# ScalarE's tanh of the last merge tile, moved ahead of the next tile's first attention step

## The chip, the cores and the metric

One core of one Trainium2 chip runs the whole program. The metric is the device time of one execution in microseconds, from first to last instruction with what lies around it. The time before is the median of three runs.

## What is computed

Four transformer blocks run one after the other on one sequence of 512 tokens with 1024 features: two layers of a first kind, then two of a second kind. Only the mixer of the second kind matters here. Cut to that:

```python
def hybrid_mixer_2(h, ...):
    q_nsa, kv_nsa, g_nsa, qkv_sb, g_merge = split(h @ w_in)       # one wide input product
    o_nsa = nsa_attention(...)     # compressed blocks + selected blocks + window, softmax
    o_sb = stick_breaking_attention(...)
    g_a, g_b = split(sigmoid(g_merge), 2)
    y = g_a * (o_nsa @ w_proj_nsa) + g_b * (o_sb @ w_proj_sb)
    return y @ w_out

def stick_breaking_attention(q, k, v):       # for blocks of 128 queries
    z = q @ k.T * scale
    log_1m = where(strict, -softplus(z), 0)
    later = reversed_cumsum(log_1m) - log_1m
    w = where(strict, exp(log_sigmoid(z) + later), 0)
    out = w @ v
```

The kernel computes sigmoid(g) as half of 1 + tanh(g / 2): ScalarE stores the tanh in `gm`, the merge stage adds the 1 and the factor 0.5.

## The kernel before, in words

**Weights.** All weight matrices come as a stream of tiles of 128x1024. SP's queue loads a tile into a ring of four (`raw`). Products are done in three passes over pairs of rounded numbers: ScalarE copies half a tile into a rounded head `wh` (`head`, L171), GpSimd subtracts that from the raw weights for the residual `wl` (`rest`, L182), and TensorE does head x head, head x low, residual x head (L199 to L201). `wh` and `wl` hold two tiles, so the head of tile t+2 can be written, half by half, only when TensorE is done with that half of tile t (`slot_done`).

**The second mixer.** Its input product has 48 tiles (`for t in range(IN2)` in each engine's function). The last 16, t = 32 to 47, are the merge gates. Each fills a bank of 128x512 in PSUM, 4 or 5 by turns. When a merge tile t-1 is complete, VectorE multiplies its bank in place by the inverse norm (`weigh`, L2412), and ScalarE then takes the tanh into `gm` (`gate`, L2188), which frees the bank for tile t+1.

**Attention between the tiles.** Attention is cut into 52 steps: softmax attention, then four steps of the compressed blocks, then 16 stick-breaking steps. A tile has two slots, one behind its first and one behind its second half, and each slot does a part of several steps: TensorE computes the scores of step n (L2006), the transposes of the weights of step n-2 (L2027) and the values of step n-3 (L2060). In its slot n ScalarE copies the transposed weights of n-2 to SBUF (L2171), which frees banks 2 and 3, and computes two pairs of Sigmoids of the scores of n (L2149 and L2152), whose second of each pair frees score bank 0 or 1. GpSimd masks these (L1930), VectorE scans them (L2317) and multiplies (L2324). The stick-breaking steps lie in the slots of tiles 36 to 43; tile 44 has transposes, copies and values of the last two. A copy in a slot waits also for the values of n-3.

**What sets the order.** Each engine's order is written out in program order and each waits by semaphores. TensorE's iteration t is: claim the bank, first half, slot, second half, slot. VectorE's is: `weigh(t - 1)`, slot, slot, with splits of finished attention features inside the slots. ScalarE's iteration t is: first head of tile t+2, first slot, second head, tanh of merge tile t-1, second slot. The tanh waits for `inverted`, which `weigh` raises, and from the 14th merge tile on also for all stick-breaking products.

Of the kernel before, what the change touches and what calls it, by code (L numbers as in the profile page):

```python
# [203 lines left out]
def build(nc, a, out):  # L204
# [1612 lines left out]
    def second_mixer(sems, t0, joint):  # L1817
# [8 lines left out]
        kinds = MIX2_KINDS  # L1826
# [87 lines left out]
        def head_col(k, one):  # L1914
            _, tb, kind, p = steps[k]
            return 16 * tb + 8 * kind + soft_head(one, p)[2]
# [211 lines left out]
        def scalar(act):  # L2128
            def soften(k):
                kind, tb, one_, p = steps[k]  # L2130
                w_ = (tb + 1) * P
                if kind == "cmp":
                    act.wait_ge(cshift, tb + 1)
                    act.activation(csb[:, tb, :, 0:NCMP], csb[:, tb, :, 0:NCMP], ACT.Exp, scale=HD ** -0.5)\
                       .then_inc(cexp, 1)
                    return
                for one in range(2):
                    i = first_item[k] + one
                    if kind == "soft":
                        at = head_col(k, one)  # L2140
                        act.wait_ge(bank_free[one], score_use[k, one])
                        act.activation(prs[i % 6][:, 0:w_], prs[i % 6][:, 0:w_], ACT.Exp, bias=mins[:, at:at + 1],
                                       scale=-1.0, accum_out=den[:, at:at + 1]).then_inc(weights, 1)
                        continue
                    n = 2 * (k - CMP) + one
                    act.wait_ge(score, i + 1)
                    if n >= 3:
                        act.wait_ge(products, n - 2)
                    act.activation(lgs[n % 3][:, 0:w_], ps[one][:, 0:w_], ACT.Sigmoid, scale=-(HD ** -0.5))\  # L2149
                       .then_inc(keeps, 1)  # L2150
                    act.wait_ge(turned, i - 5)
                    act.activation(prs[i % 6][:, 0:w_], ps[one][:, 0:w_], ACT.Sigmoid, scale=HD ** -0.5)\  # L2152
                       .then_inc(bank_free[one], 1)

            def copies(k):
                kind, tb, _, p = steps[k]
                w_ = (tb + 1) * P
                if kind == "cmp":
                    act.wait_ge(turned, first_item[k] + 1)
                    if tb >= 2:  # L2160
                        act.wait_ge(pv, first_item[k] - 1)
                    act.activation(ptc[tb % 2][0:NCMP, 0, :], ps[2][0:NCMP, :], ACT.Copy).then_inc(bank_free[2], 1)
                    return
                for one in (range(2) if kind == "sb" else (1,)):
                    i = first_item[k] + one
                    act.wait_ge(turned, i + 1)
                    if k == CMP:
                        act.wait_ge(pv, SOFT_ITEMS)
                    elif k:
                        act.wait_ge(pv, first_item[k - 1] + 2)  # L2170
                    act.activation(m.tmp[:, one, 0:w_], ps[2 + one][:, 0:w_], ACT.Copy)\  # L2171
                       .then_inc(bank_free[2 + one], 1)

            def slot(n):
                if 0 <= n - TURN_LAG < len(steps):
                    copies(n - TURN_LAG)
                if n < len(steps):
                    soften(n)
                if n == GELU_TURN:
                    act.wait_ge(gelu_in, 1)  # L2180
                    act.activation(gt[:], gu_[:], ACT.Tanh).then_inc(gelu_out, 1)

            def gate(t):
                c = kinds[t][1]
                act.wait_ge(inverted, c + 1)
                if c >= 13:
                    act.wait_ge(products, 2 * 4 * NT)
                act.activation(gm[:, c, :], ps[bank_of[t]][:], ACT.Tanh, scale=0.5)\  # L2188
                   .then_inc(bank_free[bank_of[t]], 1)

            for t in range(IN2):
                kind, c = kinds[t]
                if t == 0:
                    joint.copy_inverse(act)
                else:
                    s.head(act, t0 + t + 2, 0)
                if (t, 0) in slots:
                    slot(slots[t, 0])
                s.head(act, t0 + t + 2, 1)
                if t and kinds[t - 1][0] == "merge":  # L2200
                    gate(t - 1)
                if kind == "svalue" and c == 3:
                    s.done(act, t0 + t)
                    for tb in range(2):
                        act.activation(sv2[:, tb, :], ps[tb][:], ACT.Identity, scale=xinv4[:, tb:tb + 1]).then_inc(bank_free[tb], 1)
                    act.wait_ge(bank_free[7], 1)
                    act.activation(gts_flat, vsw[:, :, 256:280], ACT.Tanh, scale=0.5).then_inc(gates, 1)
                if kind == "compress" and c % 4 == 3:
                    kv = c // 4
                    s.done(act, t0 + t)  # L2210
                    act.activation(raw_h[0:32, kv, :], ps[4 + kv][0:32, 0:P], ACT.Copy).then_inc(hidden_copied, 1)
                    act.wait_ge(hidden_copied, kv + 1)
                    act.sem_inc(bank_free[4 + kv], 1)
                if (t, 1) in slots:
                    slot(slots[t, 1])
            gate(IN2 - 1)

        def vector(dve):
# [198 lines left out]
            for t in range(IN2):  # L2417
# [26 lines left out]
                if (t, 1) in slots:  # L2444
                    slot(slots[t, 1])
            weigh(IN2 - 1)
        stage = Stage(sync, gpsimd, tensor, scalar, vector)
        stage.feat_ready = feat_ready
        return stage
# [449 lines left out]
```

## Time and profile before

| | |
|---|---|
| median of three runs | 3118.8 us (3118.59 to 3124.26) |
| profiled execution | 3121.47 us, its span 3119.7 us |
| TensorE busy | 3023.1 us (97%) |
| TensorE weight load | 2415.5 us (77%) |
| VectorE busy | 1756.7 us (56%) |
| ScalarE busy | 1257.8 us (40%) |
| GpSimd busy | 1393.7 us (45%) |
| mean granted TensorE clock | 0.974 |

Busy shares are of the span and an average over all stages. The ends of TensorE's products are modelled, so its busy time is not time at its peak. An engine's idle time is listed with the instruction that came after it and with what released that.

### The profile page before, as it was taken

The numbers are of one execution on the slowest core, as the hardware profiler recorded it, in microseconds if no ns is written. First come the engines' busy times: TensorE is split into PE (matmuls) and PEld (weight loads), VectorE is DVE, ScalarE is ACT, GpSimd is POOL, SyncE is SP. The second block draws the span as 40 slices with busy tenths as digits, with TensorE's granted clock in tenths as the row PEclk, the third lists the DMA queues.
The fourth block names the chain that finished last, engine by engine and source line by source line (L and its number), as shares of the span: only waits on it lengthen the run. The fifth ranks groups of instructions, "written<-read, shape, count | busy, mean of one in ns | idle before, by whom it ended". The sixth has DMA issues, their size and how long they took to land.

```text
span 3119.7 us, 40188 instructions
## 1 busy us (share of the span) xinstructions
PE 3023.1 (97%) x14910; PEld 2415.5 (77%) x14910; DVE 1756.7 (56%) x3049; ACT 1257.8 (40%) x2459; POOL 1393.7 (45%) x1184
## 2 busy tenths in 40 slices
PE   6998999999999999999999999999999999999998
PEld 5766788888776778888867678888887677888886
DVE  7786856623796554223385746665246666576621
ACT  3445432233445432233354535444344444354432
POOL 2341355545432254445542545544464335454443
PEclk9998899998999899999999999999999999999999
DMA  5422456622420122322421122222232211222222
GB/s 221 132 82 75 149 202 232 245 93 75 132 84 28 41 92 95 101 93 83 132 89 48 48 82 81 102 95 100 100 115 90 70 55 55 95 88 95 96 94 74
DMA packets 92978, 316.55 MB, mean 101 GB/s; under 512 B 12016, under 2 KB 12656, under 8 KB 92656
## 3 DMA queue, kind: packets, MB, share of 16 engines
q1 hardware_dynamic: 92784, 313.99, 29.2%
q8 instruction: 119, 1.95, 0.3%
q14 instruction: 75, 0.61, 0.1%
HBM read 301.36 MB, written 2.10 MB: 97 GB/s over the span
## 4 chain that ended last, share of the span: by engine, by line
PE 90%; DVE 7%; ACT 1%; issue 1%; DMA 0%; POOL 0%; SPq 0%; DVEq 0%; ACTq 0%
PE bank L199 24%; PE bank L200 23%; PE bank L201 23%; PE bank L2006 2%; PE bank L2027 2%; PE bank L2060 2%; DVE sel L1521 1%; DVE small L1520 1%; PE bank L1288 1%; PE bank L429 1%; DVE qk L1577 1%; PE bank L430 1%; PE bank L433 1%; PE bank L2108 1%; PE bank L2109 1%
## 5 line engine op out<-in xcount | busy, mean ns | idle before, releaser
L182 POOL TENSOR_TENSOR wl<-raw,wh 128x512 fp32r<-128x512 f32 (+1 forms) x952 | 1254.8, 1322 | 1547.3 <-ACT wh L171 1546.7
L171 ACT ACTIVATE wh<-raw 128x512 fp32r<-128x512 f32 (+1 forms) x952 | 587.5, 623 | 1302.4 <-PE bank L201 1209.9
L199 PE MATMUL bank<-hh,wh 128*128 128x512 f32 x2368 | 945.7, 399 | 10.4 <-ACT gm L2188 4.8
L201 PE MATMUL bank<-hh,wl 128*128 128x512 f32 x2368 | 926.1, 391 | 0.0
L200 PE MATMUL bank<-hl,wh 128*128 128x512 f32 x2368 | 926.0, 391 | 0.0
L199 PEld LDWEIGHTS bank<-hh,wh 128*128 128x128 f32 x2368 | 446.5, 189 | 136.0 <-issue 32.7
L201 PEld LDWEIGHTS bank<-hh,wl 128*128 128x128 f32 x2368 | 446.6, 189 | 95.4
L200 PEld LDWEIGHTS bank<-hl,wh 128*128 128x128 f32 x2368 | 447.0, 189 | 89.9 <-issue 0.5
L201 PE MATMUL bank<-hidh,wl 128*128 128x512 f32 x704 | 273.9, 389 | 0.0
L199 PE MATMUL bank<-hidh,wh 128*128 128x512 f32 x704 | 273.9, 389 | 0.0
L200 PE MATMUL bank<-hidl,wh 128*128 128x512 f32 x704 | 273.9, 389 | 0.0
L392 DVE TENSOR_TENSOR bank<-x,y 128x512 f32<-128x512 f32 x49 | 59.8, 1220 | 294.0 <-ACT y L370 293.9
L199 PEld LDWEIGHTS bank<-hidh,wh 128*128 128x128 f32 x704 | 132.2, 188 | 27.6
L201 PEld LDWEIGHTS bank<-hidh,wl 128*128 128x128 f32 x704 | 132.2, 188 | 27.3
L200 PEld LDWEIGHTS bank<-hidl,wh 128*128 128x128 f32 x704 | 132.2, 188 | 27.3
L914 DVE TENSOR_TENSOR hidden<-gate,bank 128x512 f32<-128x512 f32 x44 | 30.1, 684 | 166.2 <-PE bank L201 156.8
L916 DVE CAST hidh<-hidden 128x512 fp32r<-128x512 f32 x88 | 119.1, 1354 | 3.0
L2171 ACT ACTIVATE tmp<-bank 128x128 f32<-128x128 f32 (+3 forms) x128 | 52.6, 437 | 132.8 <-PE bank L2060 132.3
L881 DVE TENSOR_TENSOR bank<-bank,acc 128x512 f32<-128x512 f32 x88 | 61.5, 699 | 71.8 <-PE bank L201 66.6
L866 DVE SCALAR_TENSOR_TENSOR up<-bank,pc,up 128x511 f32<-128x511 f32 x88 | 65.9, 749 | 38.9 <-ACT up L846 37.3
L866 DVE SCALAR_TENSOR_TENSOR gate<-bank,pc,gate 128x511 f32<-128x511 f32 x88 | 65.9, 749 | 38.9 <-ACT gate L846 37.3
L398 DVE TENSOR_TENSOR acc<-bank,acc 128x512 f32<-128x512 f32 x48 | 32.6, 680 | 85.5 <-ACT bank L375 85.5
(427 smaller groups left out, 4225.7 us busy)
## 6 DMA issues: line engine op xcount, KB each, us to landing
raw<-in_w SPq DMA_DIRECT2D x444, 512.0 KB, 3.4
mod_raw2a<-in_wmod SPq DMA_DIRECT2D x28, 512.0 KB, 4.6
mod_raw2b<-in_wmod SPq DMA_DIRECT2D x28, 512.0 KB, 4.8
raw<-in_w SPq DMA_DIRECT2D x32, 384.0 KB, 2.9
first_mods<-in_wmod SPq DMA_DIRECT2D x16, 512.0 KB, 13.8
mod_raw<-in_wmod SPq DMA_DIRECT2D x12, 512.0 KB, 3.5
out_raw<-in_wmod SPq DMA_DIRECT2D x12, 512.0 KB, 5.5
tmp<-rawb SPq DMA_DIRECT2D x72, 64.0 KB, 2.4
```

The lines of the kernel that those rows point to most:

```text
L171: act.activation(self.m.wh[:, t % 2, w_], self.m.raw[:, t % RING, w_], ACT.Copy)\
L182: pool.tensor_tensor(self.m.wl[:, t % 2, w_], self.m.raw[:, t % RING, w_], self.m.wh[:, t % 2, w_].bitcast(F32), ALU.subtract)\
L199: pe.matmul(out, wh, xh, start=start, stop=False)
L200: pe.matmul(out, wh, xl, start=False, stop=False)
L201: return pe.matmul(out, wl, xh, start=False, stop=stop)
L392: dve.tensor_tensor(dst, m.x[:, nb, :], m.y[:, nb, :], ALU.mult).then_inc(cross_ready, 1)
L866: return dve.scalar_tensor_tensor(buf[:, pair, shift:T], bank[:, 0:T - shift], m.pc[:, col:col + 1], buf[:, pair, shift:T], ALU.mult, ALU.add)
L881: dve.tensor_tensor(bank[:], bank[:], joint.inverse, ALU.mult).then_inc(normed, 1)
L916: step(dve.tensor_copy(hidh[:, q, :], hs[:, pair, :]))
L2006: pe.matmul(ps[one][:, 0:w_], q_, k_, start=True, stop=True).then_inc(score, 1)
L2027: ins = pe.transpose(ps[2 + one][:, kb * P:(kb + 1) * P], prs[i % 6][:, kb * P:(kb + 1) * P], ident)
L2060: ins = pe.matmul(feature_of(bank, h), v_, m.tmp[:, one, kb * P:(kb + 1) * P], start=first, stop=last)
```

## The change

In ScalarE's function of the second mixer the call of `gate(t - 1)` moves from behind the second weight head to behind the first one, ahead of the first attention slot. The tanh of tile 47, after the loop, stays where it is.

```diff
@@ -2194,11 +2194,11 @@
                     joint.copy_inverse(act)
                 else:
                     s.head(act, t0 + t + 2, 0)
+                if t and kinds[t - 1][0] == "merge":
+                    gate(t - 1)
                 if (t, 0) in slots:
                     slot(slots[t, 0])
                 s.head(act, t0 + t + 2, 1)
-                if t and kinds[t - 1][0] == "merge":
-                    gate(t - 1)
                 if kind == "svalue" and c == 3:
                     s.done(act, t0 + t)
                     for tb in range(2):
```

## Rows read from the trace of the kernel before

**Rows 1.** Windows of tiles 39 to 47, both layers: us, then each engine's busy us
```profile
1744.00:1830.00 86.00, 83.59 (x487) 60.26 (x486) 61.49 (x72) 42.63 (x92) 44.85 (x60) 1.00 0.17 58
2564.00:2650.00 86.00, 83.59 (x487) 60.30 (x486) 61.20 (x71) 42.88 (x93) 44.64 (x58) 1.00 0.17 58
```

**Rows 2.** Timeline, tiles 45 and 46: start us, us, engine, line, operation [idle before]
```profile
1808.19 0.63 ACT L171 ACTIVATE wh<-raw 128x512 fp32r<-128x512 f32 x1 [1.83 <-PE bank L201]
1813.27 0.50 PE L199 MATMUL bank<-hh,wh 128*128 128x512 f32 x1 [1.21 <-ACT gm L2188]
```

**Rows 3.** Waits from 1670 to 1860: who waited for what: us, times, longest
```profile
PE bank L199 <- ACT gm L2188: 2.4, 2, 1.2
```

**Rows 4.** Line of the tanh: count, duration in ns, first and last start
```profile
L2188 ACT ACTIVATE gm<-bank x32: 578/580/642, 1686.9 to 2646.6; 128x512 f32<-128x512 f32 x32
```

**Rows 5.** Timeline, tile 39: copies, last Sigmoid, weigh, next scores
```profile
1746.49 0.66 ACT L2171 ACTIVATE tmp<-bank 128x256 f32<-128x256 f32 x2 [1.00 <-PE bank L2060]
1747.83 0.43 ACT L2152 ACTIVATE pr<-bank 128x256 f32<-128x256 f32 x1
1747.75 0.70 DVE L2412 TENSOR_TENSOR bank<-bank,acc 128x512 f32<-128x512 f32 x1
1749.24 0.70 PE L2006 MATMUL bank<-sk,sq 64*128 64x256 f32 x4
```

**Rows 6.** Timeline, tile 40, the same four
```profile
1756.23 0.66 ACT L2171 ACTIVATE tmp<-bank 128x256 f32<-128x256 f32 x2 [1.43 <-PE bank L2060]
1757.89 0.53 ACT L2152 ACTIVATE sq<-bank 128x384 f32<-128x384 f32 x1
1757.65 0.70 DVE L2412 TENSOR_TENSOR bank<-bank,acc 128x512 f32<-128x512 f32 x1
1758.97 0.92 PE L2006 MATMUL bank<-sk,sq 64*128 64x384 f32 x4
```

**Rows 7.** Timeline: copies and first scan of one slot, first scan of tile 39
```profile
1741.93 0.45 ACT L2171 ACTIVATE tmp<-bank 128x128 f32<-128x128 f32 x2 [0.35 <-PE bank L2060]
1743.30 1.63 DVE L2317 TENSOR_TENSOR_SCAN lg<-lg,eps 128x256 f32<-128x256 f32 x2 [0.19 <-POOL lg L1930]
1748.36 0.68 DVE L2317 TENSOR_TENSOR_SCAN turn<-turn,eps 128x256 f32<-128x256 f32 x1
```

**Rows 8.** Timeline, tile 41, the four of rows 5
```profile
1766.38 0.87 ACT L2171 ACTIVATE tmp<-bank 128x384 f32<-128x384 f32 x2 [1.64 <-PE bank L2060]
1768.25 0.54 ACT L2152 ACTIVATE pr<-bank 128x384 f32<-128x384 f32 x1
1766.89 0.68 DVE L2412 TENSOR_TENSOR bank<-bank,acc 128x512 f32<-128x512 f32 x1
1769.12 0.92 PE L2006 MATMUL bank<-sk,sq 64*128 64x384 f32 x4
```

**Rows 9.** Timeline, tile 43, and scores of tile 42 for comparison
```profile
1780.18 1.25 PE L2006 MATMUL bank<-sk,sq 64*128 64x512 f32 x4
1789.14 1.09 ACT L2171 ACTIVATE tmp<-bank 128x512 f32<-128x512 f32 x2 [2.41 <-PE bank L2060]
1790.03 0.69 DVE L2412 TENSOR_TENSOR bank<-bank,acc 128x512 f32<-128x512 f32 x1
1791.89 1.47 PE L2006 MATMUL bank<-sk,sq 64*128 64x512 f32 x4
```

**Rows 10.** Timeline, tile 44: copies, weigh (of two tiles), transposes of the second slot
```profile
1800.39 1.09 ACT L2171 ACTIVATE tmp<-bank 128x512 f32<-128x512 f32 x2 [1.29 <-PE bank L2060]
1802.75 1.28 DVE L2412 TENSOR_TENSOR bank<-bank,acc 128x512 f32<-128x512 f32 x2
1803.09 1.03 PE L2027 MATMUL bank<-cst,pr 128*128 128x128 f32 x8
```

**Rows 11.** Timeline: one shape of product, twice
```profile
1770.25 1.56 DVE L2324 TENSOR_TENSOR pr<-pr,lg 128x383 f32<-128x383 f32 x1
1771.73 0.54 DVE L2324 TENSOR_TENSOR pr<-pr,turn 128x383 f32<-128x383 f32 x1
```

## The prediction

> **What bounds the kernel now.** I read the windows of the stage first, then the timeline of each engine in it, then who waits for the tanh. Times are us from the start of the span, for the first of the two layers of the second kind; T39 is input tile 39 of that mixer (the merge tiles are T32 to T47), "first half" and "second half" are TensorE's four chunks (of three products each) before and after the first attention step.
>
> [Rows 1] are the windows of T39 to T47 in both layers. TensorE is busy 83.59 of 86.00 us in either, at a granted clock of 1.00 (the 2.4 GHz level), VectorE about 61, ScalarE about 43. So a microsecond that TensorE waits here is a microsecond of the kernel, and the two layers repeat each other: I work one out and double it. That VectorE is not full says nothing of how late its work is when ScalarE asks for it, and this is what the change turns on.
>
> [Rows 2, 3] show what the tanh costs now. TensorE's tile T46 needs the bank that the tanh of T44 reads. That tanh stands behind the weight head that waits for all of T45. T46's first product starts at 1813.27, after 1.21 us in which TensorE is idle and that the tanh ends. The row of waits has two of these in the layer, 2.4 us; the other stands before T47. Earlier merge tiles have attention work on TensorE between two tiles, which covers the tanh.
>
> **The change, part by part.** *Moved forward:* the tanh of T(t-1), now behind ScalarE's first weight head of iteration t and ahead of the first attention step. Its own work is 0.58 us [rows 4], neither added nor removed: 30 of the 32 tanhs are moved, the last of each layer stays. No DMA is issued by it; SP's and GpSimd's queues keep their order.
>
> *What it gains.* T44's tanh can go after the head at 1808.19 [rows 2]: 1808.19 + 0.63 + 0.58 = 1809.40, well ahead of the end of T45's products (1813.27 - 1.21 = 1812.06). The tanh of T45 likewise. Both waits go: 2 x 1.21 = 2.42 us a layer. What is next late there is nothing: GpSimd's residual of the next tiles has more than one tile of time.
>
> *What it costs: a wait.* The tanh waits until VectorE has multiplied the same bank (weigh, L2412). VectorE does that at the head of its own iteration t, but it gets to iteration t only when it has done all of the second attention step of t-1. Where ScalarE's tanh stood until now, the wait was always over (no wait on it in the trace). In its new place, queued behind it are on ScalarE: the copies of the first attention step (L2171), its four Sigmoids (L2149, L2152) and the second weight head. TensorE waits for these Sigmoids, since they free the two score banks that the scores of the next step (L2006) claim.
>
> So for each tile there are two numbers. *Delay* of the attention step: end of weigh + 0.58 - start of the copies now. *Cover*: the time between the last Sigmoid's end and TensorE's claim of the second bank, which is half-way through the L2006 group. What TensorE loses is delay less cover.
>
> T39 [rows 5]: weigh ends 1747.75 + 0.70 = 1748.45; delay 1748.45 + 0.58 - 1746.49 = 2.54. Last Sigmoid ends 1748.26; the second score group starts 1749.24 + 0.35 = 1749.59; cover 1.33. Loss 1.21.
>
> T40 [rows 6]: weigh ends 1758.35; 1758.35 + 0.58 - 1756.23 = 2.70. But VectorE is behind more than TensorE by then: copies to first scan are 1743.30 - 1741.93 = 1.37 [rows 7], so the scan of T39 starts at 1749.03 + 1.37 = 1750.40 and not 1748.36, 2.04 later, and VectorE runs without a pause up to weigh. TensorE is 1.21 later, the rest, 0.83, is added: delay 3.53. Cover 1759.43 - 1758.42 = 1.01. Loss 2.52.
>
> From here on TensorE's lateness carries over: the second step's copies start that much later, and VectorE, which then waits for these, reaches weigh that much later. Both sides move alike, and the formula holds on the old times.
>
> T41 [rows 8]: 1767.57 + 0.58 - 1766.38 = 1.77; cover 1769.58 - 1768.79 = 0.79. Loss 0.98. T42 repeats this pattern (one more tile, rows not shown); I take 0.98 again.
>
> T43 [rows 9]: 1790.72 + 0.58 - 1789.14 = 2.16. Here the scores took 1.47 where the same four products took 1.25 at 1780.18: TensorE already waits 0.2 for a Sigmoid, cover 0. Loss 2.16.
>
> T44 [rows 10]: no Sigmoids any more; the transposes of the second step (L2027) need the banks that the copies free. Weigh ends 1803.44 (1802.75 + 0.69); 1803.44 + 0.58 - 1800.39 = 3.63. The copies now end 1801.48, the second bank is claimed at 1803.09 + 0.5 = 1803.59: cover 2.1. Loss 1.52.
>
> Before T39 the wait costs nothing by the same reading (rows not shown): VectorE has reached weigh by the end of ScalarE's first weight head, and the shorter Sigmoids there leave more cover than the 0.58 us. From T45 on there is no attention step to delay.
>
> Sum: 1.21 + 2.52 + 0.98 + 0.98 + 2.16 + 1.52 = 9.37 us lost, 2.42 gained, net 6.95 a layer, 13.9 for both. The profiled execution took 3121.5 (span 3119.7): 3135.4 by it. The median of the runs is 3118.8, 2.7 below: 3118.8 + 13.9 = **3132.7 us**, slower by 0.4%.
>
> **Bounds of what the trace doesn't show.** The new wait itself is in no row. From below: VectorE's chain from scans to weigh may become shorter, since GpSimd's residual falls elsewhere in it. The same product took 1.56 at one time and 0.54 at the other [rows 11]. Where a residual no longer meets a product, weigh comes 1.02 earlier. Once a tile from T40 on, with the losses cut at 0: 1.21 + 1.50 + 0 + 0 + 1.14 + 0.50 = 4.35, net 1.9 a layer, 3.9 in all: 3122.7. From above: one more product a tile meets a residual: 9.37 + 5 x 1.02 = 14.47, net 12.05 a layer, 24.1 in all: 3142.9. I take the phases as they are, since the residual of the second head follows the last Sigmoid by nearly as much as before.
>
> By the Trainium skill ("SBUF — State Buffer", section "SBUF: two separate sides") the pair of ports that VectorE and GpSimd share is an exclusive lock, held for a whole instruction, so that the later one is blocked rather than slowed. [Rows 11] agree in kind: 1.56 against 0.54 for one shape. By that rule the chain could only change by whole blocks, which leads to the same two ends and not to a new sum.
>
> **Rivals.** *A, the wait bites* (the forecast): 3132.7.
>
> *B, the wait is there and TensorE does not feel it* (other side): VectorE catches up. ScalarE's delay pushes the Sigmoids, but were each delay below its cover, only the two bank waits would remain as an effect: -4.8, 3114.0. For it: VectorE is idle 25 of 86 us, and cover is 1.33 to 0.79 in T39 to T41. Against it: delays are 1.77 to 3.53 in these tiles, and in T43 there is no cover. It decides where weigh ends less than cover less 0.58 us behind the copies' start of today, 0.2 to 0.75 us in T39 to T41; it ends 1.2 to 2.1 us behind them there.
>
> *C, the wait bites, but the loop shortens* by the missing collisions of the lower bound: +3.9, 3122.7. For it: ScalarE's second head no longer has a tanh behind it, and the residual can start somewhat earlier against VectorE's scans. Against: the moves are some tenths, a product lasts more than a microsecond.
>
> *D, more collisions*: up to 3142.9.
>
> **How the numbers follow.** A 0.70, C 0.13, B 0.08, D 0.09. Around A I allow 3 us a layer for covers that I read only from half of a group's time: 3126 to 3138. The range takes in D in most part and the upper part of C: 3123 to 3140. 0.2% of the kernel is 6.2 us, about what a measurement can tell here. Slower by more: A and D, 0.79, and the top of C, 0.01. Within: the rest of C, 0.12, and 0.03 of B, whose own working ends inside this bound. Faster by more: 0.05, a B with somewhat more than the two bank waits in it.
>
> **What would show it.** In the profile after: ScalarE idle before L2188 and released by VectorE's L2412, about 1 to 3 us each in T39 to T44; TensorE's L2006 idle and released by ScalarE's L2152 (or L2149) in the second steps of T39 to T43, and L2027 by L2171 in T44, some 9 us a layer together; no wait of L199 on L2188 any more; VectorE's weigh of T43 about 8 us later than before. The number of tanhs and their 0.58 us unchanged. It would be wrong if TensorE's scores still start without a wait in T39 to T42 (then B), or if the tanh never waits for VectorE. If the waits are there and each is about a microsecond smaller, it is C.

## The result and the profile after

The changed kernel took 3142.78 us (median of six runs, 3137.23 to 3152.78), the kernel before 3123.2 us in its six (3118.59 to 3124.85): ratio 1.0062, 95% interval 1.0047 to 1.0077, 19.6 us slower. The forecast was +13.9 us. The direction and the chain of waits came out; the size is 1.4 times what I worked out, and the time lies 2.8 us above the range.

Single runs of one program scatter by up to 25 us here, mostly ahead of this stage: in the profiles of this study its first scores start anywhere between 1686.1 and 1704.7 us. The stage itself is far steadier. I call *stretch* the time from the first scores of the compressed blocks (first L1992, slot of T34) to the first product of the merge stage (first L199 with `fnh`). It holds all the moved tanhs but that of T32. Between the two stretches 685.8 to 687.6 us pass, whichever the kernel, and two profiles of one program (e7 and e11) differ there by 1.2 us. Windows cut to it, before and then after, both layers (columns: window, its length, then busy us and instructions of TensorE products, weight loads, VectorE, ScalarE, GpSimd, granted clock, DMA share, GB/s):

```profile
1692.32:1825.82 133.50, 131.04 (x853) 96.13 (x853) 93.19 (x148) 62.77 (x147) 63.45 (x91) 1.00 0.15 52
2511.91:2645.41 133.50, 131.05 (x853) 96.16 (x853) 93.18 (x148) 62.77 (x147) 63.63 (x91) 1.00 0.15 52
```
```profile
1694.82:1839.18 144.36, 138.43 (x854) 100.12 (x853) 91.68 (x148) 62.81 (x148) 64.32 (x91) 0.96 0.15 48
2526.80:2669.77 142.97, 136.82 (x853) 99.06 (x853) 91.60 (x148) 62.79 (x148) 64.62 (x91) 0.98 0.15 49
```

The stretch grew by 10.9 and 9.5 us, 20.3 together, which is the 19.6 us of the medians within their interval (15 to 24 us). The instructions are the same. TensorE is idle 5.9 and 6.2 us in it (2.5 before), and is *busy* 7.4 and 5.8 us longer with the same work. Part of that has its reason in the third column from the end: the granted clock, 1.00 in both layers before, is 0.96 and 0.98. Two decimals are coarse for a spell of a few us; where I give the length of a spell below, it is from the trace's own record of the granted clock.

Who waits, in the first and the second layer (us in total, times, longest), where [rows 3] had the one wait for the tanh:

```profile
ACT gm L2188 <- DVE bank L2412: 18.3, 5, 4.3
PE bank L2006 <- ACT sq L2152: 3.4, 2, 2.0
PE bank L2006 <- ACT pr L2152: 1.4, 2, 0.9
PE bank L2027 <- ACT tmp L2171: 1.2, 1, 1.2
...
ACT gm L2188 <- DVE bank L2412: 19.3, 6, 4.3
PE bank L2006 <- ACT sq L2152: 3.4, 2, 2.0
PE bank L2006 <- ACT pr L2152: 1.4, 2, 0.9
PE bank L2027 <- ACT tmp L2171: 1.3, 1, 1.3
```

The tanh now waits for VectorE's weigh, and TensorE's scores for the Sigmoids queued behind it. The wait of L199 for the tanh is gone. T40 shows the chain of it, ScalarE then VectorE then TensorE (start us, us, engine, line [idle before <- released by]; `...` marks lines left out); it answers to [rows 6]:

```profile
1758.17 0.63 ACT L171 ACTIVATE wh<-raw 128x512 fp32r<-128x512 f32 x1 [1.18 <-PE bank L201]
1763.06 0.60 ACT L2188 ACTIVATE gm<-bank 128x512 f32<-128x512 f32 x1 [4.26 <-DVE bank L2412]
1763.55 0.65 ACT L2171 ACTIVATE tmp<-bank 128x256 f32<-128x256 f32 x2
...
1762.33 0.70 DVE L2412 TENSOR_TENSOR bank<-bank,acc 128x512 f32<-128x512 f32 x1
...
1765.03 1.98 PE L2006 MATMUL bank<-sk,sq 64*128 64x384 f32 x4 [1.99 <-ACT sq L2152]
1766.93 1.11 PE L2027 MATMUL bank<-cst,pr 128*128 128x128 f32 x4
1767.98 1.12 PE L2060 MATMUL bank<-tmp,sv 128*64 128x128 f32 x8
1769.03 0.80 PE L199 MATMUL bank<-hh,wh 128*128 128x512 f32 x1
1769.62 0.63 PE L200 MATMUL bank<-hl,wh 128*128 128x512 f32 x1
1770.05 0.63 PE L201 MATMUL bank<-hh,wl 128*128 128x512 f32 x1
1770.48 0.63 PE L199 MATMUL bank<-hh,wh 128*128 128x512 f32 x1
```

ScalarE has its weight head done at 1758.8 and stands until 1763.06: 4.3 us, where I had put each of these waits at 1 to 3 us. What I had not forecast is in the last lines: after 1.99 us of idleness TensorE's products follow one another every 0.43 us and take 0.63, where the same product takes 0.39 elsewhere in this trace and the next starts after 0.23. The clock column of two windows of 20 us says the same, behind T40 and behind T43:

```profile
1763.00:1783.00 20.00, 18.01 (x87) 11.92 (x87) 12.32 (x15) 10.82 (x27) 9.29 (x15) 0.83 0.11 33
1806.00:1826.00 20.00, 18.84 (x128) 14.24 (x127) 11.63 (x13) 8.09 (x16) 8.48 (x10) 0.91 0.16 54
```

The clock has two levels, so a mean of 0.83 over 20 us is 6.8 us at the lower one (1.2 GHz), and 0.91 is about 3.4 us. The spells of the stretch are 6.8 and 3.4 us in the first layer, 3.4 and 3.4 in the second.

Step by step, how far TensorE lags behind the kernel before (start of the same group, each from the first L1992; us gained or lost in that tile, second layer, where the low spells are short):

| | forecast | after, second layer | of it at low clock |
|---|---|---|---|
| T39 | 1.21 | 1.46 | 0 |
| T40 | 2.52 | 4.41 | 1.5 |
| T41 | 0.98 | 0.00 | 0 |
| T42 | 0.98 | 1.39 | 0 |
| T43 | 2.16 | 3.68 | 1.6 |
| T44 | 1.52 | 1.57 | 0 |
| both bank waits | -2.42 | -3.04 | 0 |
| sum | 6.95 | 9.47 | 3.1 |

### The profile page after: what moved, and what is told of

It is laid out like the page before. It is cut to its first block, busy times and chain, and to the rows that moved or that the text cites. A ratio compares the mean times of both kernels' runs of the same rounds, so it can differ in the third digit from the quotient of the medians.

```text
span 3144.5 us, 40188 instructions
## 1 busy us (share of the span) xinstructions
PE 3043.0 (97%) x14910; PEld 2430.5 (77%) x14910; DVE 1756.0 (56%) x3049; ACT 1257.0 (40%) x2459; POOL 1393.0 (44%) x1184
## 4 chain that ended last, share of the span: by engine, by line
PE 86%; DVE 8%; issue 3%; ACT 2%; POOL 1%; DMA 0%; SPq 0%; DVEq 0%; ACTq 0%; POOLq 0%
PE bank L199 22%; PE bank L201 22%; PE bank L200 22%; PE bank L2006 2%; PE bank L2027 2%; PE bank L2060 2%; PE bank L1288 1%; DVE sel L1521 1%; PE bank L429 1%; DVE small L1520 1%; PE bank L430 1%; PE bank L433 1%; DVE qk L1577 1%; PE bank L2108 1%; PE bank L2109 1%
## 5 line engine op out<-in xcount | busy, mean ns | idle before, releaser
L199 PE MATMUL bank<-hh,wh 128*128 128x512 f32 x2368 | 946.5, 400 | 4.9 <-POOL wl L182 3.6
L199 PEld LDWEIGHTS bank<-hh,wh 128*128 128x128 f32 x2368 | 447.1, 189 | 127.9 <-issue 32.3
L199 PE MATMUL bank<-hidh,wh 128*128 128x512 f32 x704 | 273.9, 389 | 0.0
L199 PEld LDWEIGHTS bank<-hidh,wh 128*128 128x128 f32 x704 | 132.1, 188 | 27.5
```

The costliest lines, as they stand in the source:

```text
L199: pe.matmul(out, wh, xh, start=start, stop=False)
```

## The experiments

Stretches below are of the first and the second layer of one profile each.

**e1 and e2: the two halves of the change.** e1 makes the tanh early only where no attention step is behind it, e2 only where one is.

```diff
-                if t and kinds[t - 1][0] == "merge":
+                if t and kinds[t - 1][0] == "merge" and kinds[t - 1][1] >= 12:    # e2: < 12
                     gate(t - 1)
                 if (t, 0) in slots:
                     slot(slots[t, 0])
                 s.head(act, t0 + t + 2, 1)
+                if t and kinds[t - 1][0] == "merge" and kinds[t - 1][1] < 12:     # e2: >= 12
+                    gate(t - 1)
```

> The tanh goes ahead of the first attention step only for T44, T45 and T46 (behind it, as before, for T32 to T43). Theory (the two bank waits are the whole gain, the wait for VectorE's weigh in T39 to T44 the whole loss): no wait of TensorE for a tanh, none for a Sigmoid beyond those of before; the stretch from the first scores of the compressed blocks to the first merge product, 133.5 us per layer before, gets 2.4 to 2.7 shorter, 131.0; the time 5 us below before (-0.15%). Rival (the tanh's place costs something of its own wherever it stands, or the clock loses even without a wait): the stretch stays at 133 or more.

Measured: 3119.29 us against 3124.05, ratio 0.9985 (0.9969 to 1.0000); stretches 130.51 and 130.51, no wait of TensorE for a Sigmoid or a tanh, clock 1.00. So the gain is 3.0 us a layer, more than the 2.4 to 2.7 expected. By the times alone it is just at the edge of what can be told; the stretch is clear.

> The tanh goes ahead for T32 to T43 and stays behind for T44 to T46. Theory: the loss alone. The kernel after had stretches of 144.4 and 143.0 us against 133.5; here both bank waits of 1.2 come back: about 146.5 and 145, the time some 5 us above the kernel after (+25 us, +0.8% on before). TensorE's idle waits for Sigmoids and copies sum to about 6 us a layer, and the granted clock falls to its lower level in the stretch, which it never does in it before; waits and low clock together explain the loss. Rival (the low clock has another cause than the waits): no fall in the stretch although the waits are there, and a loss of 6 us a layer only.

Measured: 3146.23 us, ratio 1.0074 (1.0050 to 1.0097); stretches 146.13 and 145.95, clock 0.98 in both, the same waits as after plus the two bank waits. The loss alone is 12.6 and 12.5 us a layer. The clock is low for 6.8 us in each of its layers. Gain and loss add up to the kernel after: 12.6 - 3.0 = 9.6 (after: 10.9 and 9.5; the 1.4 more in the first layer is one longer low spell).

**e3 and e4: take away the wait.** e3 keeps the early tanh and moves what it waits for; e4 puts the tanh behind the Sigmoids, still ahead of the second head.

```diff
# e3, VectorE's function, on top of the change
             for t in range(IN2):
-                if t and kinds[t - 1][0] == "merge":
-                    weigh(t - 1)
...
+                if kind == "merge":
+                    weigh(t)
                 if (t, 1) in slots:
                     slot(slots[t, 1])
-            weigh(IN2 - 1)
```
```diff
# e4, ScalarE's function
                 if (t, 0) in slots:
                     slot(slots[t, 0])
+                if t and kinds[t - 1][0] == "merge":
+                    gate(t - 1)
                 s.head(act, t0 + t + 2, 1)
```

> The kernel after, and VectorE's weigh of a merge tile moved too: from the head of VectorE's next iteration to ahead of its own second attention step (the bank is complete by then). Theory (ScalarE's tanh waits for weigh because weigh stands behind a whole attention step on VectorE): the tanh no longer waits, no wait of TensorE for Sigmoids beyond those of before, no fall of the clock in the stretch, stretch 131 us, time 5 us below before. Rival 1 (the tanh's own 0.58 us ahead of the copies delays the Sigmoids): still a few tenths of wait in T41 to T43 and a stretch of 133 to 135. Rival 2 (weigh now ahead of the scans delays VectorE's products by 0.6 us and TensorE's transposes): waits of L2027 on L2324.

Measured: 3111.83 us, ratio 0.9968 (0.9955 to 0.9982): faster than both kernels, and clear of noise. Against the kernel before it gains 12.2 us in the medians; the two stretches explain 6.2 of them, which lies within the interval (6 to 14 us), and nothing here shows a cause for the rest. The windows of its stretches show a TensorE without a gap:

```profile
1687.52:1817.96 130.44, 130.44 (x854) 96.26 (x853) 94.06 (x148) 63.16 (x148) 64.05 (x91) 1.00 0.16 53
2503.80:2634.18 130.38, 130.38 (x853) 96.30 (x853) 93.99 (x148) 63.14 (x148) 64.31 (x91) 1.00 0.16 53
```

The tanh stands in the same early place as in the kernel after, and nobody waits for it or behind it. So neither its place nor its 0.58 us cost anything; the loss is the wait for weigh. Both rivals fall: no wait of L2027 on L2324 was added either.

> The tanh stands behind the first attention step and ahead of the second weight head. Theory: it still waits for VectorE in T39 to T43, by 0 to 1 us since weigh ends about when the Sigmoids end, but behind it stands only the second weight head, which TensorE needs a tile later, and the next copies, which wait for TensorE anyway. So no loss, and T44's to T46's tanh is early: stretch 131 us, time 5 us below before. Rival (any wait of ScalarE for VectorE in these tiles reaches TensorE): waits of TensorE on L2171 or L2152 and a stretch above 134.

Measured: 3118.37 us, ratio 0.9976 (0.9960 to 0.9992); stretches 130.39 and 130.38. The tanh still waits for VectorE, once long, and TensorE does not feel it (waits of the first layer):

```profile
ACT gm L2188 <- DVE bank L2412: 2.2, 2, 2.0
```

Two things differ from the kernel after. The tanh is asked for later, so nearly all of its wait is gone: 2.2 us in the layer for 18.3. And the one long wait that is left, 2.0 us in T44, has a weight head next behind it; TensorE is idle 0.00 us in the stretch. This run does not tell what a wait of 4 us ahead of a weight head would do.

**e9: weigh first alone.** The edit of e3 on the kernel before.

> Weigh first on VectorE, with the tanh left behind the second head as before. Theory (weigh's place is worth nothing by itself; in the kernel with both moves it only takes away the wait): the bank waits of 1.2 us before T46 and T47 stay, stretch 133.5 as before, time as before within 0.1%. Rival (part of what weigh first gave was its own): stretch below 133.

Measured: 3122.71 us, ratio 0.9988 (0.9971 to 1.0005); stretches 133.55 and 133.54. As forecast, weigh's place is worth nothing without the early tanh.

**e10, e5, e6: one tile at a time.** These, e7, e11 and e8 have one run each, so only their stretches are read, not their times. From the kernel before, with `kinds[t - 1][1] == 6`, `== 7` or `== 10` as the condition for the early tanh.

> From the kernel before, only T39's early tanh (that of merge tile 38). Waits alone: 1.21 by my working, 1.5 by the kernel after; stretch 135.0, no fall of the clock. VectorE is 2.04 us late behind it (0.83 more than TensorE), but nobody asks for weigh early in T40, so no further loss. Rival (VectorE's lateness reaches TensorE by the products too): a wait of L2027 and a stretch above 135.5.

Measured: stretches 135.15 and 135.12, +1.6; one wait of L2006 of 0.9 us; clock 1.00.

> From the kernel before, only T40's early tanh (that of merge tile 39); all others stay behind the second head. Waits alone: the delay is 2.70 and the cover 1.01 us, so TensorE loses 1.7 us and the stretch goes from 133.5 to 135.2. Theory (waits and, after them, TensorE at its lower clock): the scores' wait of 1.7 us, and behind it spaced-out products at half speed, 1.5 to 3 us more, stretch 136.5 to 138.5 and a fall of the granted clock in it. Rival (the clock falls only when several tiles lose time one after the other): 135.2 and no fall.

Measured: 135.72 and 135.64, +2.2; one wait of 1.3 us; clock 1.00. The theory missed here: no fall came, and the stretch is within 0.5 of the rival's 135.2. A wait of this length does not always bring the lower clock.

> From the kernel before, only T43's early tanh (that of merge tile 42). Waits alone: 2.16 us, stretch 135.7. Theory: 1.5 us more for the lower clock, 137, with a fall of the granted clock. Rival as for T40 alone: 135.7 and no fall.

Measured: 138.79 and 137.20. Both layers have the same wait of 1.4 us for a Sigmoid (L2006 on L2152). The windows of the stretches differ in the clock, and by 1.6 us in length:

```profile
1695.21:1834.00 138.79, 134.95 (x854) 98.18 (x853) 93.26 (x148) 62.88 (x147) 62.88 (x91) 0.98 0.16 50
2520.49:2657.69 137.20, 133.37 (x854) 97.51 (x853) 93.17 (x148) 62.75 (x147) 63.42 (x91) 0.99 0.15 51
```

The trace has a low spell of 6.8 us in the first and of 3.4 us in the second. Here the waits are T43's 2.16 of my working and the rest, 3.1 and 1.5 us, is the clock.

**e7, e11 and e8: a wait without VectorE.** On e3, in which nothing waits, ScalarE does more tanhs of the same bank, one after the other, in T40 only.

```diff
             def gate(t):
                 c = kinds[t][1]
                 act.wait_ge(inverted, c + 1)
                 if c >= 13:
                     act.wait_ge(products, 2 * 4 * NT)
+                if c == 7:
+                    for i in range(6):          # e8: 4
+                        act.activation(gm[:, c, :], ps[bank_of[t]][:], ACT.Tanh, scale=0.5).then_inc(hidden_copied, 1)
+                        act.wait_ge(hidden_copied, 3 + i)
```

> The kernel with weigh first, stretch 130.4, and at T40's tanh six more of the same tanh one after the other on ScalarE, each waiting for the one before (about 0.65 us each, 3.9 us), so that the Sigmoids of T40 are late by ScalarE's own work and by no wait for VectorE. Free time ahead of the copies 0.85, cover 1.0: TensorE waits about 2.1 us. Theory (TensorE's idle time itself brings the lower clock, whoever causes it): stretch 130.4 + 2.1 + 1.5 to 3 = 134 to 135.5, the clock falls behind T40. Rival (the low clock belongs to the wait for VectorE, or to VectorE's changed work): 132.5, no fall.

Measured: 135.75 and 132.62.

> The same program as e7, run again. There the first layer had a stretch of 135.75 with 6.8 us at the lower clock and the second 132.62 with none, for the same wait. If the fall is a matter of chance or of when the wait comes, each layer shows again either 132.6 or about 1.6 us more for each 3.4 us at the lower clock. If it belongs to the first layer's place in the program, the two layers come out as they did.

Measured: 134.18 and 132.66. The windows of the four stretches, e7 and then e11:

```profile
1699.28:1835.03 135.75, 134.35 (x854) 98.47 (x854) 93.13 (x148) 66.51 (x154) 63.80 (x91) 0.97 0.16 51
2522.44:2655.06 132.62, 131.22 (x854) 96.60 (x853) 93.89 (x148) 66.51 (x154) 64.17 (x91) 1.00 0.16 53
```
```profile
1696.55:1830.73 134.18, 132.78 (x854) 97.57 (x853) 93.16 (x148) 66.52 (x154) 63.81 (x91) 0.99 0.15 52
2516.97:2649.63 132.66, 131.26 (x854) 96.54 (x853) 93.92 (x148) 66.53 (x154) 64.04 (x91) 1.00 0.15 53
```

TensorE is idle 1.40 us in each of the four, and its wait is the same. Where the clock stayed up, the stretch is 2.2 us longer than e3's. With 3.4 us at the lower level (first layer of e11) it is 1.5 us longer still, with 6.8 us (first layer of e7) 3.1 us. That is the clean price of a low spell. It came here behind a wait that VectorE had no part in. The length of the first layer's spell differed between two runs of one program, so the place does not fix the length. Whether it fixes that a spell comes is left open: both came in the first layer, none in the second.

> As before with four more tanhs instead of six (2.6 us): TensorE waits about 0.8 us in T40. Theory: as in T39 and T42 of the kernel after, where 1.4 to 1.5 us of wait came without a fall, only the wait is lost: stretch 131.2, no fall. Rival (every wait brings a low stretch with it): above 132.

Measured: 131.64 and 131.40, clock 1.00: 1.2 and 1.0 us for a wait put at 0.8, no fall. As in T39 and T42 of the kernel after. The trace shows only 0.14 us of idle time for it; the rest lies inside the group of the scores, as explained below for T39.

## Why the forecast was right or wrong, point by point

**The mechanism** is the one forecast, shown from both sides: the tanh waits for weigh (5 and 6 waits of up to 4.3 us), the Sigmoids wait behind it, TensorE's scores wait for these; with weigh moved away (e3) all of it is gone, with the tanh behind the Sigmoids (e4) most of the wait goes and all of the loss. Rival B is out. So is D, although its end, 3142.9, lies beside the measured 3142.8: it needed more collisions of VectorE with GpSimd and 14.5 us of waits a layer, and VectorE's busy time in the stretch fell instead, from 93.2 to 91.7 and 91.6 us. That its number fits is chance.

**The sum of the waits** came out close, in part by luck: 9.37 a layer forecast. Measured, stretch less the kernel before, plus the gain of 3.06, less the price of the low spells from e7 and e11 (3.1 for 6.8 us, 1.55 for 3.4): 144.36 - 133.50 + 3.06 - 4.7 = 9.2 in the first layer, 142.97 - 133.50 + 3.06 - 3.1 = 9.4 in the second. Only 5.9 and 6.2 of it are idle time of TensorE, where I had expected some 9 of it to show as idle. Within the sum, errors cancelled:

- T39, T40 and T42 cost 0.3 to 0.5 more than worked out. T39 alone 1.6 for 1.21 (e10), T40 alone 2.2 for 2.70 - 1.01 = 1.69 (e5). The reason is in the *cover*: I let TensorE claim the second bank half-way through the L2006 group. The single records of the kernel before have the first products of the two banks start together, T39's at 1749.24 and 1749.25, so the second bank is wanted at the start of the group. Behind a wait they cannot: each bank's two products start when its own Sigmoid is done, the first bank's at 1752.66 and the second bank's at 1753.22, behind the Sigmoid that ends at 1753.17. The group then takes 1.25 us for the 0.70 of [rows 5]:

```profile
1752.66 1.25 PE L2006 MATMUL bank<-sk,sq 64*128 64x256 f32 x4 [0.93 <-ACT pr L2152]
1752.72 0.44 ACT L2152 ACTIVATE pr<-bank 128x256 f32<-128x256 f32 x1
```

  With the cover taken to the start of the group the same rows give T39 2.54 - 0.98 = 1.56 (measured 1.46, alone 1.6), T40 alone 2.70 - 0.55 = 2.15 (2.1 and 2.2), T40 3.53 - 0.55 = 2.98 (4.4 less 1.5 for the clock), and 0.46 more in T42: 1.44 (1.39).
- T41 cost nothing, for 0.98. "Both sides move alike" failed in that place: VectorE reached weigh sooner than TensorE reached T41. Before T41's tanh, in the kernel after:

```profile
1771.95 1.02 DVE L2317 TENSOR_TENSOR_SCAN lg<-lg,eps 128x384 f32<-128x384 f32 x1
1772.89 0.53 DVE L2324 TENSOR_TENSOR pr<-pr,turn 128x383 f32<-128x383 f32 x1
1773.34 0.55 DVE L2324 TENSOR_TENSOR pr<-pr,lg 128x383 f32<-128x383 f32 x1
1773.81 0.69 DVE L2412 TENSOR_TENSOR bank<-bank,acc 128x512 f32<-128x512 f32 x1
...
1774.03 0.63 ACT L171 ACTIVATE wh<-raw 128x512 fp32r<-128x512 f32 x1 [2.61 <-PE bank L201]
1774.57 0.58 ACT L2188 ACTIVATE gm<-bank 128x512 f32<-128x512 f32 x1
```

  The product of 0.53 is the one that takes 1.64 at this point of the kernel before, together with GpSimd's residual. It looks like rival C's mechanism, but it is an effect of the low clock. In the six layers with a low spell behind T40 (after, e2, the first ones of e7 and e11) no product of this step meets the residual; in all others one does and takes 1.55 to 1.65. e11 has both in one program, the first layer with the spell, the second without:

```profile
1771.97 0.53 DVE L2328 TENSOR_TENSOR pr<-pr,turn 128x383 f32<-128x383 f32 x1
2591.74 1.56 DVE L2328 TENSOR_TENSOR pr<-pr,turn 128x383 f32<-128x383 f32 x1
```

  (L2328 is L2324 of the kernel before.) With TensorE at the lower clock ScalarE's head and with it the residual come later, 4.4 for 3.6 us behind the copies in e11, and TensorE comes later to T41 as well, while VectorE's own work takes no longer. So a spell behind T40 also saved what T41 would have cost, 1.77 - 0.33 = 1.4 by the corrected cover, which is an estimate. T43's 2.16 (2.1 measured, e6's second layer 3.7 less 1.55) and T44's 1.52 (1.57) stood.

**The gain** was undersized: 2.42 forecast, 2.99 measured in e1 (133.50 - 130.51); in e3 the stretch is another 0.07 shorter ahead of T39, which makes the 3.06 above. The idle time in a row starts where the last product ends by the profile, 0.39 us behind its start, while the next would have started after 0.23: so a wait of 1.21 us idle is worth 1.5.

**The step that failed** is "What TensorE loses is delay less cover". It leaves out a second part, TensorE's own slower work behind the wait, and puts it at nothing without a reason. I read a granted clock of 1.00 in [rows 1] and took it for given; it was so in a stage in which TensorE never stood for over 1.2 us. The lower clock cost 4.7 and 3.1 us in the two layers. That is 7.8 of the 20.3 us by which the stretches grew; waits less gains are the other 12.5 (this split is made with the prices of e7 and e11 and is no second proof of them). T41's saving has to be set against it: without any spell I would put the loss at 12.5 + 2 x 1.4, about 15 us, which is an estimate that no run checks. The second fault, in the size alone, is the cover, 0.3 to 0.5 us a tile in T39 to T42.

**The range**, 3123 to 3140, was missed by 2.8 us. Two things lie behind that, and each is larger than the miss: the clock term, and the start. Six runs of the kernel before had a median of 3123.2, where the three that I started from had 3118.8. I bounded the collisions of GpSimd and VectorE from both sides and the clock from none. As a rival it would have had a place: 3 to 9 us more for both layers, by the spells seen since.

**What stays open:** which waits bring the lower clock. Over all profiles, none of the 29 waits of TensorE of 1.16 to 1.34 us in the stretches was followed by a spell, 7 of the 11 of 1.38 to 1.43 us were, and all four of 2.0 us. The 1.4 us in T43 alone (e6) brought one in both layers, the 1.4 us in T40 (e7 and e11) in two cases of four. So longer waits bring it more often, but length alone does not tell equal ones apart, and no run here was made to find what does.

## What to carry to other kernels

Before an instruction is moved forward in an in-order queue, ask where its producer stands in *its* queue, and what is queued behind the new place: the tanh's waits cost 12.5 us a layer with copies and Sigmoids queued behind it (e2, the clock included), and behind the Sigmoids, where little of the wait was left and only a weight head stood behind it, nothing (e4). If the early place is wanted, move the producer forward as well (e3). When two banks are claimed by one group of products, ask when each product starts, not only when the group does. And a wait of the engine that bounds the kernel has to be priced with a margin for the clock: here 1.5 to 3 us behind a wait of 1.4 us, in 7 cases of 11.

## What the runs showed of the hardware

- TensorE, at the upper clock throughout a stage, fell to the lower level behind a single wait of 1.40 us in two of four equal cases (e7, e11), for 3.4 or 6.8 us, which cost 1.5 or 3.1 us.
- Waits up to 1.34 us were never followed by a fall in these stretches (29 cases), waits of 2.0 us always (4 cases).
- A bank wait of 1.21 us idle was worth 1.50 us when it was taken away (e1).
- First score products of two banks, of 64 rows each, start within 0.01 us of one another where both banks are free; a group of four then takes 0.70 us, and 1.25 us where the second bank comes free later (T39 before and after).
- A VectorE product of 128x383 takes 0.53 to 0.55 us alone and 1.55 to 1.65 where it meets GpSimd's residual; the clock of TensorE decided in e11 which of the two it was.
- A kernel with no wait at all left in the stage (e3) and one with a wait on ScalarE that nobody feels (e4) have the same stretch to 0.05 us.
